# Starting the output projection inside the stage that makes its input, in two stages of a two-block model on one core

## The reference

```python
def nsa_mixer(x, w_in, w_out, shared):             # second layer of the first block
    proj = x @ w_in
    ...                                            # q, z and gates; three attentions
    y = jnp.sum(gate[..., None] * o * jax.nn.silu(z), axis=2).reshape(bsz, seq, ATTN_WIDTH)
    return y @ w_out
...
x = layer_norm(DEEPNORM_ALPHA * x + y, ln_g[layer], ln_b[layer])
...
mix = jnp.concatenate([o_a.reshape(b, s, A_WIDTH), o_b.reshape(b, s, B_WIDTH)],
                      axis=-1).astype(x.dtype)     # two gated, normalised mixers
h = h + mix @ w_out[l]
hn = _rmsnorm(h, ffn_norm_g[l])
h = h + _peer(hn, peer_w_query[l], peer_sub_keys[l], peer_u[l], peer_v[l])
return _rmsnorm(h, final_norm_g)
```

## Time and profile before

| | |
|---|---|
| median of 3 runs | 3216.97 us (3216.86 to 3219.8) |
| the profiled execution | 3213.72 us |
| its span | 3211.9 us, mean granted clock of PE 0.973 |
| PE busy | 3064.9 us, 95% of the span |
| PE weight loads (PEld) busy | 2513.7 us, 78% |
| DVE, ACT busy | 2156.2 us (67%), 1498.5 us (47%) |
| DMA | 529.91 MB, 165 GB/s on the mean |
| the queue of SP and ACT loads (q1) | 49.2% of 16 engines' time |

### The profile page before, as it was taken

How to read it: one execution, slowest core, us unless ns; L and a number is a source line. 1 busy time by engine, 2 the same in 40 slices (tenths; PEclk the granted TensorE clock), 3 DMA queues, 4 the chain that set the end, 5 groups by cost and what they waited for, 6 DMA issues and landing times.

```text
span 3211.9 us, 60302 instructions
## 1 busy us (share of the span) xinstructions
PE 3064.9 (95%) x23922; PEld 2513.7 (78%) x23922; DVE 2156.2 (67%) x3061; ACT 1498.5 (47%) x2021; POOL 38.4 (1%) x37
## 2 busy tenths in 40 slices
PE   7798999999987989999989999999999999999998
PEld 6695999989976879998989888777777777777654
DVE  8676444555556775566479998777777777777645
ACT  5433433566643533463444487444444444444444
POOL 1000000000000110000000000000000000000000
PEclk9779999999998999999999999999999999999999
DMA  6224655444444432443565524555565565565564
GB/s 212 73 90 163 230 173 181 148 140 140 138 158 142 161 105 93 132 152 112 197 202 178 173 93 151 191 199 192 187 202 192 185 202 191 187 201 189 189 206 149
DMA packets 143961, 529.91 MB, mean 165 GB/s; under 512 B 16992, under 2 KB 17760, under 8 KB 142048
## 3 DMA queue, kind: packets, MB, share of 16 engines
q1 hardware_dynamic: 141120, 515.57, 49.2%
q10 hardware_dynamic: 2592, 10.68, 0.9%
HBM read 521.99 MB, written 4.19 MB: 164 GB/s over the span
## 4 chain that ended last, share of the span: by engine, by line
PE 38%; DVE 10%; DMA 1%; issue 1%; ACT 0%; DVEq 0%; SPq 0%; ACTq 0%
PE ps L2548 21%; PE ps L2479 16%; DVE mem L236 3%; DVE mem L2819 2%; DVE mem L2822 1%; DMA mem<-weights 1%; DVE mem L2337 0%; DVE mem L2338 0%; DVE mem L2809 0%; DVE mem L2340 0%; DMA mem<-experts 0%; DVE mem L2339 0%; DVE mem L2779 0%; DVE mem L2782 0%; DVE mem L2784 0%
## 5 line engine op out<-in xcount | busy, mean ns | idle before, releaser
L236 DVE TENSOR_TENSOR mem<-mem,rounded 128x1024 bf16<-128x1024 f32 x952 | 1154.4, 1226 | 732.6 <-ACT rounded L230 724.7
L230 ACT CAST rounded<-mem 128x1024 fp32r<-128x1024 f32 x952 | 992.3, 1047 | 1372.3 <-PE ps L2548 336.0
L263 PE MATMUL ps<-rounded 128*128 128x256 f32 x3328 | 471.9, 291 | 34.4 <-DVE mem L236 30.7
L263 PEld LDWEIGHTS ps<-rounded 128*128 128x128 f32 x3328 | 420.7, 192 | 39.7 <-DVE mem L236 16.7
L263 PE MATMUL ps<-mem,rounded 128*128 128x256 bf16 x3328 | 428.3, 276 | 17.6 <-DVE mem L236 17.6
L263 PE MATMUL ps<-rounded,mem 128*128 128x256 bf16 x3328 | 441.6, 278 | 0.0
L263 PEld LDWEIGHTS ps<-mem,rounded 128*128 128x128 bf16 x3328 | 318.3, 99 | 65.3 <-DVE mem L236 17.5
L263 PEld LDWEIGHTS ps<-rounded,mem 128*128 128x128 bf16 x3328 | 314.9, 97 | 60.3 <-issue 1.4
L2548 PE MATMUL ps<-rounded 128*128 128x512 f32 x1024 | 335.7, 441 | 2.1 <-DVE mem L2866 2.1
L2848 DVE TENSOR_TENSOR mem<-mem,ps 128x512 f32<-128x512 f32 x392 | 268.2, 684 | 65.5 <-PE ps L2548 58.5
L2548 PE MATMUL ps<-mem,rounded 128*128 128x512 bf16 x1024 | 307.3, 382 | 0.0
(11 more groups left out here) (428 smaller groups left out, 2416.4 us busy)
## 6 DMA issues: line engine op xcount, KB each, us to landing
mem<-experts SPq DMA_DIRECT2D x512, 512.0 KB, 3.6
mem<-weights SPq DMA_DIRECT2D x440, 512.0 KB, 3.6
mem<-x_t SPq DMA_DIRECT2D x4, 512.0 KB, 10.4
mem<-x_rows SPq DMA_DIRECT2D x1, 2048.0 KB, 8.4
mem<-cmp_w_k ACTq DMA_DIRECT2D x4, 512.0 KB, 6.2
mem<-cmp_w_v ACTq DMA_DIRECT2D x4, 512.0 KB, 4.7
h_rows<-mem SPq DMA_DIRECT2D x1, 2048.0 KB, 7.2
mem<-h_rows ACTq DMA_DIRECT2D x1, 2048.0 KB, 7.8
```

The lines of the kernel that those rows point to most:

```text
L230: self.nc.scalar.copy(self.parts(c % SLOTS)[0], self.raw(c % RAW)).then_inc(self.high_done, 1)
L236: self.nc.vector.tensor_tensor(wl, self.raw(c % RAW), wh.bitcast(F32), ALU.subtract).then_inc(self.low_done, 1)
L263: mm = self.nc.tensor.matmul(self.ps[:, bank, half * 256:half * 256 + 256], a, b, start=(part == 0 and n == 0), stop=(part == PIECES - 1 a ...
```

## The change

`project_residual` becomes a class `Residual` whose pieces are called by the two stages themselves, inside their own Blocks, and no Block follows for it. Per stage:

- ACT makes the high parts of the projection's first three pieces, and the first three copies of turned banks, ahead of the last drain and silu. DVE makes the low parts of both kinds ahead of the last gates.
- The turned banks go to PSUM banks 3 to 7 only (`Y_BANKS`, `MIX_BANKS`), three of them used twice, so that banks 0 to 2 stay the tiles'. A second use waits until the low part of the first is made.
- PE multiplies part 0 of the projection's first tile as soon as two turned banks have low parts, and places parts 1 to 3 between and after the remaining transposes.
- A copy over the old activations' high part waits for the last old piece that reads that quarter (`k.multiplied`).
- The first tile's fourth piece and the other seven tiles follow in the old order.

In the second mixers the transposes are put in another order (`MIX_TURN`), because the columns of bank 3 are gated last.

```diff
+class Residual:
...
+    def pieces(self, j):
+
+        at = PIECES * (self.first + j)
+        return range(at + (0 if j else RAW), at + PIECES)
...
+    def part(self, pe, part, low, value):
+        pe.wait_ge(low, value)
+        self.k.piece(pe, PIECES * self.first + part, self.act, "token")
+
+    def multiply(self, pe):
+        self.k.multiply(pe, self.first + 1, self.n - 1, self.act, "token")
+
+    def first_high(self, act):
+        for c in range(RAW):
+            self.k.high(act, PIECES * self.first + c)
+
+    def first_low(self, dve):
+        for c in range(RAW):
+            self.k.low(dve, PIECES * self.first + c)
...
@@ attention
+    Y_BANKS = (3, 4, 5, 6, 7, 3, 4, 5)
...
             k.stream(sp, AT_B_OUT)
+            tail.fetch(sp, AT_IN2)
...
             turn_rows(6, 3)
             turn_rows(7, 4)
-            pe.wait_ge(k.bank_free, drained(N_ATT - 1))
+            tail.part(pe, 0, low, 2)
             pe.wait_ge(y_ready, n_steps - 4)
-            turn_rows(0, 5)
-            turn_rows(1, 6)
+            turn_rows(3, 5)
+            turn_rows(4, 6)
+            tail.part(pe, 1, low, 4)
             pe.wait_ge(y_ready, n_steps)
-            turn_rows(2, 7)
+            pe.wait_ge(low, 3)
+            turn_rows(5, 7)
+            tail.part(pe, 2, low, 6)
+            tail.part(pe, 3, low, 8)
+            tail.multiply(pe)
...
+            def y_high(j):
+
+
+                act.wait_ge(full, j + 1)
+                act.wait_ge(k.multiplied, first + n_pieces - 3 + j // 2)
+                nc.scalar.copy(mh[:, j * BANK:(j + 1) * BANK], ps[:, Y_BANKS[j], :]).then_inc(split, 1)
+
+            tail.first_high(act)
+            for j in range(3):
+                y_high(j)
             drain(N_ATT - 1)
             silu(HEADS // 2 - 1, 2, 3)
...
+            for j in range(3, 8):
+                y_high(j)
+            tail.high(act)
...
+            tail.first_low(dve)
+            for j in range(3):
+                y_low(j)
             dve.wait_ge(z_ready, HEADS // 2 + 1)
             for i in range(n_steps - 4, n_steps):
                 gated(i, 2, 3)
...
+            for j in range(3, 8):
+                y_low(j)
+            tail.low(dve)
@@ second mixers
+    MIX_TURN, MIX_BANKS = (0, 1, 2, 4, 5, 3, 6, 7), (4, 5, 6, 7, 3, 4, 5, 6)
...
+            for i in range(4):
+                turn_mix(i)
+            upto(n_pieces)
+            turn_mix(4)
+            tail.part(pe, 0, low, 2)
+            for i in range(5, 8):
+                turn_mix(i)
+            tail.part(pe, 1, low, 6)
+            tail.part(pe, 2, low, 6)
+            tail.part(pe, 3, low, 8)
+            tail.multiply(pe)
...
+            tail.first_high(act)
+            for i in range(3):
+                mix_high(i)
+            drain(N_IN2 - 1)
+            for i in range(3, 8):
+                mix_high(i)
+            tail.high(act)
...
+            for n in range(3):
+                gates_of(n)
+            tail.first_low(dve)
+            for i in range(3):
+                mix_low(i)
+            gates_of(3)
+            for i in range(3, 8):
+                mix_low(i)
+            tail.low(dve)
```

More of the change, by code:

```diff
@@ L346, in low_turned @@
                                      ALU.subtract).then_inc(low, 1)
[L348 to L416, removed]
@@ L439, in rms_scale, with __init__, drained, fetch @@
                                               in1=g, op0=ALU.mult, op1=ALU.mult), signal)
+class Residual:
+    def __init__(self, k, first, n, act, x, scale, dst, stats, loads):
+        self.k, self.first, self.n, self.act, self.x, self.scale, self.dst = k, first, n, act, x, scale, dst
+        self.stats, self.loads = stats, loads
+        self.rows_in, self.squared = k.sem(f"rows_in_{first}"), k.sem(f"squared_{first}")
+    def pieces(self, j):
+        at = PIECES * (self.first + j)
+        return range(at + (0 if j else RAW), at + PIECES)
+    def drained(self, j):
+        return self.first + j + 1 + BANKS
+    def fetch(self, sp, upto):
+        for i, (to, name, layer) in enumerate(self.loads):
+            self.k.stream(sp, self.first + 2 + 2 * i, ahead=False)
+            src = self.k.ins[name]
+            sp.dma_start(to, src if layer is None else src[layer]).then_inc(self.rows_in, 16)
+        self.k.stream(sp, upto)
+        sp.wait_ge(self.rows_in, 16 * len(self.loads))
+    def part(self, pe, part, low, value):
[9 more added lines that the diff above has]
+            self.k.low(dve, PIECES * self.first + c)
+    def high(self, act):
+        k, n = self.k, self.n
+        a = k.stepper(act, k.astep)
+        def squares(j):
+            act.wait_ge(k.bank_free, self.drained(j))
+            for tt in range(TT):
+                at = tt * D + j * 256
+                a(k.nc.scalar.activation(self.stats[:, 64:320], self.dst[:, at:at + 256], ACT.Square,
+                                         accum_out=self.stats[:, n * tt + j:n * tt + j + 1]), self.squared)
+        for j in range(n):
+            for c in self.pieces(j):
+                k.high(act, c)
+            if self.scale == 1.0 and j >= 2:
+                squares(j - 2)
+        if self.scale == 1.0:
+            squares(n - 2)
+        k.nc.scalar.activation(k.spare[:, 4:6], k.spare[:, 0:2], ACT.Sqrt)
+        if self.scale == 1.0:
+            squares(n - 1)
+    def low(self, dve):
+        k, n = self.k, self.n
+        v = k.stepper(dve, k.vstep)
+        def rows(a, j):
+            return a.rearrange("p (a n) -> p a n", a=TT)[:, :, j * 256:(j + 1) * 256]
+        for j in range(n + 1):
+            if j < n:
+                for c in self.pieces(j):
+                    k.low(dve, c)
+            if j:
+                t = self.first + j - 1
+                dve.wait_ge(k.multiplied, PIECES * (t + 1))
+                k.nc.vector.scalar_tensor_tensor(
+                    out=rows(self.dst, j - 1), in0=rows(self.x, j - 1), scalar=self.scale,
+                    in1=k.ps[:, t % BANKS, :].rearrange("p (a n) -> p a n", a=TT), op0=ALU.mult,
+                    op1=ALU.add).then_inc(k.bank_free, 1)
+                if self.scale != 1.0:
+                    dve.wait_ge(k.bank_free, self.drained(j - 1))
+                    for tt in range(TT):
+                        at = 6 * n * tt + 6 * (j - 1)
+                        own = tt * D + (j - 1) * 256
+                        v(k.nc.vector.bn_stats(self.stats[:, at:at + 6], self.dst[:, own:own + 256]))
@@ L1466, in _ @@
                 gated(i, 2, 3)
[L1467 to L1472, removed]
+            for j in range(3, 8):
+                y_low(j)
+            tail.low(dve)
 def first_block(k):
     s5_mixer(k)
[L1478 to L1481, removed]
+    attention(k)
 BDK = 128
@@ L1599, in _ @@
             k.stream(sp, AT_OUT2)
+            tail.fetch(sp, AT_WQ)
         @block.tensor
@@ L1778, in _, with turn_mix @@
                 upto(AT_CHUNKS + CHUNK_GAP * (cc + 1))
[L1779 to L1787, removed]
+            def turn_mix(i):
+                b = MIX_TURN[i]
+                if b < 4:
                     pe.wait_ge(gated, 2 + TT * (b + 1))
+                if i >= 5:
+                    pe.wait_ge(low, i - 4)
                 for c in range(2):
@@ L2291, in _, with gates_of @@
             upto(n_pieces)
-            for n in range(4):
+            def gates_of(n):
                 dve.wait_ge(k.bank_free, drained(24 + n))
```

34 lines of the change are left out of this document (23 added, 11 removed).

## The result

The changed kernel takes 3196.12 us (median of 4 runs, 3191.77 to 3197.5) against 3216.91 before (4 runs, 3215.5 to 3219.8). The ratio is 0.9936, 95% interval [0.9923, 0.9949]: 20.8 us less, 16 to 25 by the interval. The forecast was 3196.7. The profiled execution took 3197.5, with a span of 3195.7, where the forecast for it was 3193.5. One execution of the changed kernel in a later group took 5134.7 us at a mean granted clock of 0.554 and is left out of every median and ratio here.

The account below looks back on a forecast made before the run. PE, with work in 95% of the span, was taken as the bound, leaving only its idle time and slow clock to win; attention 11.5 + second mixers 8.75 = 20.25 us off 3216.97 gave 3196.7 us, range 3192 to 3205.

Parts of the forecast that it names:

- The holes and who fills them: Before each projection: PE idle 2.47 and 7.12 us in attention, 0.89 and 6.80 in second mixers; early work removes them.
- The two new waits: PE ahead of part 1 and piece 131 in attention, about 0.35 and 0.25 us; ahead of part 1 in mixers, 0.6.
- The slow clock: Projection's first three pieces run partly at 1.2 GHz behind the hole, costing 2.80 us in attention, 1.71 in mixers.
- The loads: Attention's projection: piece 134 loads later and competes with `ln_g`, a stall of 0 to 1.6 us, taken as 0.25.
- The lead: How far piece loads run ahead of need in attention's projection: 5.2 us before, spent by the change; 134 2.4 ahead.
- The sum: Both stages: attention 11.5 us plus second mixers 8.75 gives 20.25 less; everything behind each projection moves with it.
- the sign of a wrong sum: Anywhere else in the program: a stage changing by over 2 us would show the summed gain wrong.
- The loads' rival: Loads take the wait over where `ln_g` competes: 5.0 us lost, 3201.5; chance 0.11.
- The clock's rival: Short waits and alternating banks between pieces drop PE's clock in both stages: 16.4 us lost, 3213.1; chance 0.04.
- only the long one brought it down: At attention's end, the 2.47 us hole left the granted clock at 1.00; only the long hole lowered it.
- The rival that nothing but the boundary goes: Parts still wait for all low parts; each stage saves only first high and low, 2.7 us: 3211.6; chance 0.03.
- the slower one: Ring of three raw buffers never regains a lead, PE waits every piece: 32 us lost, 3228.7; chance 0.03.

Follow-up runs that it names:

- Parts late: Changed kernel, but PE multiplies parts 0 to 2 of the first tile only after the last transpose and all low parts: 3204.64 us.
- no early pieces: Changed kernel, but three pieces' high and low parts and first three copies come behind last drain, silu and gates: 3215.35 us, again 3212.0.
- holes filled: Kernel with those early parts moved back, plus unread PE transposes ahead of part 0: 3215.25 us in attention only, 3210.03 in both stages.
- mixers alone: Kernel before with the change made in the second mixers only, attention left as before: 3207.21 us, ratio 0.9969.
- gain rows together: Changed kernel, but SP loads each projection's gain rows together, right behind the load of piece 134 (118): 3202.87 us.
- one hole filled: Kernel with early pieces and copies moved back, plus 60 unread PE transposes ahead of part 0 in attention only: 3215.25 us.

## Why the prediction was right

- **The holes and who fills them.** Shown. The early highs (908.21), lows (909.36) and low parts of turned banks (912.78, done 914.66) end at the start of part 0, with no wait of PE. From the first transpose to the fourth piece I worked out 923.45 - 912.37 = 11.1 and 1518.2 - 1507.58 = 10.6; the trace has 11.2 and 10.7. The low parts that each wait names, and their order, came out as worked out. "Parts late" and "no early pieces" show that neither half does it alone.
- **The two new waits.** Predicted 0.35 and 0.25 in attention, 0.6 in the mixers; measured 0.42, 0.49 and 0.77. So my hand-offs were short by 0.07, 0.24 and 0.17.
- **The slow clock.** The rows of before gave 2.80 and 1.71 us. With holes filled the traces gave 2.7 and 1.4 to 2.9. It was right to count it, but its size was read from one execution: behind the same two holes of attention it cost only 1.3 in "mixers alone". That the one trace was near the mean of the runs is not shown.
- **The loads.** I took a stall of 0.25, in a range of 0 to 1.6. There was none: from the fourth piece to the last group of matmuls it is 1013.62 - 935.20 = 78.4 us before and 1003.47 - 925.05 = 78.4 after. The lead was as thin as worked out. The high of piece 136 starts at 934.94, so it is ready 2.35 later at 937.3 and needed at 925.01 + 13.7 = 938.7: 1.4 ahead, against the 1.6 of my bound.
- **The sum.** The distances give 11.5 + 8.6 = 20.1 us, predicted 20.25, measured 20.8 in the runs (16 to 25 by the interval). The two profiled executions differ by only 16.2: the changed one reaches the last old piece of attention 1.4 us later (913.79 against 912.37), a lateness that arises ahead of everything the change touches, takes 2.0 longer from attention's fourth piece to the last old piece of the mixers (1499.46 - 925.01 against 1507.52 - 935.10), and 0.5 longer behind the mixers' fourth piece. I had named a change of over 2 us elsewhere as the sign of a wrong sum, and this is at its edge. But a second trace of the changed kernel takes 573.5 there and "mixers alone", with the old attention, 573.4, so at least 1 us of it is the spread of executions; the rest stays open.
- **Luck.** That the medians meet within 0.6 us is luck in part. I put the profiled execution at 3193.5 and the runs' median 3.25 above it; the profile came out 4.0 higher, at 3197.5, and the median 1.4 below the profile. The four runs spread over 5.7 us.
- **Rivals.** The loads' rival needs more contention than there is ("gain rows together" makes it true, at 6.0 us). The clock's rival is refuted: the granted clock is 1.00 from 913.7 to 925, with transposes, pieces and waits of 0.4 and 0.5 us alternating, and in the mixers across the wait of 0.77; what the Trainium skill tells under "A second HAM failure mode: psum-queue depth-cycling" (page "TensorE: Matmul & The Clock Gate") did not happen here. One sentence of mine on it was too wide, though: "only the long one brought it down" holds for the kernel before, while in "parts late" two holes of 2.44 and 2.70 us with 0.42 us of work between them did it as well, and in "mixers alone" the very hole of 2.47 us was followed by the fall. The rival that nothing but the boundary goes is refuted by the rows of parts between transposes, and the slower one by the one wait of "gain rows together".

## What to carry to other kernels

A stage that ends in a chain over several engines and a next one that begins with preparing its operands are worth joining, if both things are done: the next stage's operands are prepared in the idle time of the engines that prepare them, ahead of the old stage's last waits, and the busiest engine gets next-stage work for each finished quarter of its input. Here the first alone gave about 12 of 21 us and the second alone about 2 us, within what can't be told from nothing. Count behind each hole the slow clock too, as a range of 1.3 to 2.9 us and not as one number, and check the lead of the load ring at the new start, since it is spent there first.

## What the runs showed of the hardware

The spread of one kernel's runs (3204 to 3221 for the one before) does not arise evenly over the program. Two traces of one and the same kernel (no early pieces), spans 3212.9 and 3206.7, differ by 6.8 us already at the end of attention (the part 0 rows start at 922.63 and 915.82). Windows of the two, first trace first:

```profile
100.00:200.00 100.00, 78.22 (x958) 73.76 (x957) 70.46 (x85) 34.53 (x50) 0.00 (x0) 0.68 0.11 38
```

```profile
100.00:200.00 100.00, 78.37 (x1169) 73.97 (x1167) 76.97 (x91) 34.68 (x51) 0.00 (x0) 0.74 0.11 38
```

Between 100 and 200 us, where PE runs many small matmuls with idle time between, the granted clock was 0.68 in one and 0.74 in the other, and PE got through 958 and 1169 matmuls. By 182 us one trace is 6.8 us behind the other, and it stays so to the end of attention. A change of a few us elsewhere is therefore seen best as a distance inside the trace, from a point behind that stretch.

Around the ends of the two stages, idle times of PE of 1.41 and 1.96 us with 1.3 of work between left the granted clock at 1.00; 2.44 and 2.70 with 0.4 of work between, 3.74, and all from 6.2 up brought it to 0.50. In between, the length alone does not tell. The hole of 2.47 us left it up in the kernel before and was followed by the fall in "mixers alone". The same at a third place, ahead of the same eight loads, in "no early pieces" (first) and "one hole filled":

```profile
1138.37 0.77 PEld L263 LDWEIGHTS ps<-mem,rounded 128*128 128x128 bf16 x8 [3.82 <-DVE mem L236]
```

```profile
1135.22 1.41 PEld L263 LDWEIGHTS ps<-mem,rounded 128*128 128x128 bf16 x8 [3.86 <-DVE mem L236]
```

The granted clock in the 2 us from there is 1.00 in the first and 0.50 in the second.

Transposes kept the clock up as matmuls do: 60 of them, 6.58 us in a hole of 8.1, left it at 1.00.
